# FoX and mLSTM attention steps on visible keys only, with mask and maximum in one VectorE operation

## What is computed

```python
# FoX, for one block of 128 queries
logits = jnp.einsum("bqhd,bkhd->bhqk", qi, k) * scale
logits = logits + (cum_i[..., :, None] - cum[..., None, :])
logits = jnp.where(q_pos[:, None] >= key_pos[None, :], logits, -jnp.inf)
p = jax.nn.softmax(logits, axis=-1)
...
# mLSTM; the kernel takes all 256 tokens as one chunk
dmat = cum[..., :, None] - cum[..., None, :] + ig[..., None, :]
dmat = jnp.where(causal, dmat, -jnp.inf)
m_t = jnp.maximum(inter, jnp.max(dmat, axis=-1))
s = jnp.einsum("bhtd,bhsd->bhts", qb, kb) * jnp.exp(dmat - m_t[..., None])
den = jnp.sum(s, axis=-1) + ...
h_out = num / jnp.maximum(jnp.abs(den), jnp.exp(-m_t))[..., None]
```

## Time and profile before

| | |
|---|---|
| median of three runs | 2455.86 us (2450.93, 2455.86, 2457.76) |
| profiled execution | 2448.87 us, of which the span of the trace is 2447.1 us |
| TensorE busy | 2365.3 us, 97% of the span |
| VectorE busy | 1998.9 us, 82% |
| ScalarE busy | 1032.1 us, 42% |
| mean granted TensorE clock | 0.993 of full |
| where FoX stands in the span | about 203.7 to 316.8 us |
| where mLSTM stands | about 316.8 to 386 us |

### The profile page before, as it was taken

The page is one execution under the profiler, slowest core; times in us unless marked ns, Lnnn a source line. Parts: engine busy times, 40 slices in busy tenths (PEclk is TensorE's granted clock), DMA queues, the critical chain, the costliest instruction groups (busy, mean ns, idle before and its releaser), DMA issues.

```text
span 2447.1 us, 33588 instructions
## 1 busy us (share of the span) xinstructions
PE 2365.3 (97%) x12586; PEld 2029.7 (83%) x12586; DVE 1998.9 (82%) x2707; ACT 1032.1 (42%) x1116; POOL 12.4 (1%) x23
## 2 busy tenths in 40 slices
PE   6999989899999999999989999998999999999998
PEld 6878877788888888888778888887888888888886
DVE  6779987889988888888878888877888678877875
ACT  2134444454433444344455444544444333433343
POOL 0000000000000000000000000000000000000000
PEclk9999999999999999999999999999999999999999
DMA  9999966857798667966858665565555755576553
GB/s 399 413 370 360 347 248 238 312 198 267 258 346 326 237 234 278 363 234 225 331 196 315 233 221 192 186 259 193 187 189 209 289 209 186 189 268 232 187 189 138
DMA packets 114465, 627.00 MB, mean 256 GB/s; under 512 B 12768, under 2 KB 12960, under 8 KB 63152
## 3 DMA queue, kind: packets, MB, share of 16 engines
q1 hardware_dynamic: 113648, 621.22, 68.6%
q10 hardware_dynamic: 704, 4.23, 0.4%
HBM read 623.27 MB, written 2.13 MB: 256 GB/s over the span
## 4 chain that ended last, share of the span: by engine, by line
PE 75%; DVE 14%; DMA 7%; ACT 3%; issue 1%; SPq 0%; DVEq 0%; ACTq 0%
PE bank L1825 29%; PE bank L1826 15%; PE bank L1849 9%; PE bank L1851 9%; PE bank L1850 9%; DVE lo L996 5%; DMA region<-ada_pieces 3%; DMA piece<-ada_pieces 2%; DVE piece L1007 2%; ACT hi L566 1%; PE bank L1731 1%; PE bank L1605 1%; DVE region L1007 1%; DVE y L1007 1%; DMA raw<-w_units 1%
## 5 line engine op out<-in xcount | busy, mean ns | idle before, releaser
L1825 PE MATMUL bank<-act,hi 128*128 128x512 f32 x3328 | 1172.1, 397 | 6.9 <-DVE lo L996 5.6
L566 ACT ACTIVATE hi<-raw 128x2048 fp32r<-128x2048 f32 x378 | 723.6, 1915 | 785.1 <-PE bank L1851 413.2
L1826 PE MATMUL bank<-act,lo 128*128 128x256 f32 x3616 | 1015.1, 281 | 0.0
L996 DVE TENSOR_TENSOR lo<-raw,hi 128x2048 fp32r<-128x2048 f32 x378 | 864.8, 2288 | 153.4 <-ACT hi L566 152.9
L1825 PEld LDWEIGHTS bank<-act,hi 128*128 128x128 f32 x3328 | 624.2, 188 | 159.2 <-DVE lo L996 7.0
L1826 PEld LDWEIGHTS bank<-act,lo 128*128 128x128 f32 x3616 | 685.0, 189 | 0.2
L1849 PE MATMUL bank<-hi,mid 128*128 128x512 f32 x704 | 274.5, 390 | 3.1 <-DVE lo L996 3.1
L1851 PE MATMUL bank<-hi,mid 128*128 128x512 f32 x704 | 274.0, 389 | 0.0
L1850 PE MATMUL bank<-lo,mid 128*128 128x512 f32 x704 | 274.0, 389 | 0.0
L1007 DVE SCALAR_TENSOR_TENSOR piece<-piece,cond 128x1024 f32<-128x1024 f32 x203 | 246.5, 1219 | 14.3 <-DMA piece<-ada_pieces 13.9
L1849 PE MATMUL bank<-hi,act 128*128 128x512 f32 x512 | 203.6, 398 | 6.3 <-DVE lo L996 4.0
(11 more groups left out here) (183 smaller groups left out, 1855.4 us busy)
## 6 DMA issues: line engine op xcount, KB each, us to landing
raw<-w_units SPq DMA_DIRECT2D x378, 1024.0 KB, 4.9
piece<-ada_pieces SPq DMA_DIRECT2D x203, 512.0 KB, 5.7
region<-ada_pieces SPq DMA_DIRECT2D x124, 512.0 KB, 7.9
y<-ada_pieces SPq DMA_DIRECT2D x46, 512.0 KB, 5.7
raw<-head_units SPq DMA_DIRECT2D x16, 1024.0 KB, 16.0
extra<-ada_pieces SPq DMA_DIRECT2D x11, 512.0 KB, 5.8
region<-gamma_scratch ACTq DMA_DIRECT2D x4, 1024.0 KB, 7.0
x<-x_in SPq DMA_DIRECT2D x1, 2048.0 KB, 9.4
```

What stands on the lines that cost most here:

```text
L566: sc.activation(hi[:, slot, :], raw[:, raw_slot, :], ACT.Copy).then_inc(s_hi, 1)
L996: ve.tensor_tensor(lo[:, slot, :], raw[:, raw_slot, :], hi[:, slot, :].bitcast(F32), ALU.subtract).then_inc(s_lo, 1)
L1825: pe.matmul(both, w_hi, act[:, kt, :], start=at == 0, stop=False)
L1826: i_ = pe.matmul(dst, w_lo, act[:, kt, 0:T], start=False, stop=at == DK - 1)
```

## The change

Every step of both attentions is cut to `seen(tb)` keys, 128 for token block 0 and 256 for block 1: the row product, the mLSTM scores, the mask and maximum, the exponential, the product with the scores and the scaling. (The FoX scores, the transposes and the attention products were cut already.) The row product, one matmul of 512 columns before, becomes two of 128 and 256. The mask addition and the maximum, two VectorE operations over 512 columns with a wait between them, become one `tensor_tensor_reduce` for each token block. For mLSTM its start value 0.0 takes over the `min` with 0.0 that the negation did.

```diff
-OWN = {("ff_up", None): 8, ("columns", "fox"): 4, ("values", "fox"): 8, ("columns", "mlstm"): 14,
+OWN = {("ff_up", None): 8, ("columns", "fox"): 2, ("values", "fox"): 4, ("columns", "mlstm"): 12,
...
+def seen(tb):
+
+    return (tb + 1) * P
...
-        def row_twice(k):
-
-            return extra[:, (1 + k) * T:(2 + k) * T].unsqueeze(1).broadcast_to([P, TB, T])
+        def row(k, size=T, rows=GATES):
+            return extra[0:rows, (1 + k) * T:(1 + k) * T + size]
...
-                    i_ = sc.activation(l_[:, tb, :], l_[:, tb, :], ACT.Copy, scale=column(at_ + tb))
+                    i_ = sc.activation(l_[:, tb, 0:seen(tb)], l_[:, tb, 0:seen(tb)], ACT.Copy, scale=column(at_ + tb))
...
-                                i_ = sc.activation(m_l(k)[:, tb, :], m_l(k)[:, tb, :], ACT.Exp,
-                                                   bias=column(8 * k + tb))
+                                l_ = m_l(k)[:, tb, 0:seen(tb)]
+                                i_ = sc.activation(l_, l_, ACT.Exp, bias=column(8 * k + tb))
...
-            def masked_max(l_, bank_, at_):
-
-                ve.tensor_tensor(l_, split2(bank_[:, :]), causal[:, :, :], ALU.add).then_inc(s_v, own.tick())
-                mine()
-                ve.tensor_reduce(stat[:, at_:at_ + 2], l_, AX_X, ALU.max).then_inc(s_v, own.tick())
+            def masked_max(l_, bank_, at_, least):
+
+                for tb in range(TB):
+                    i_ = ve.tensor_tensor_reduce(l_[:, tb, 0:seen(tb)], bank_[:, tb * T:tb * T + seen(tb)],
+                                                 causal[:, tb, 0:seen(tb)], 1.0, least, ALU.add, ALU.max,
+                                                 stat[:, at_ + tb:at_ + tb + 1])
+                i_.then_inc(s_v, own.tick())
                 mine()
...
-                        masked_max(m_l(k), bank[4 + 2 * k], 8 * k)
-                        ve.tensor_scalar(stat[:, 8 * k:8 * k + 2], stat[:, 8 * k:8 * k + 2], -1.0, 0.0, ALU.mult,
-                                         ALU.min).then_inc(s["mlstm_max_ready"], 1)
+                        masked_max(m_l(k), bank[4 + 2 * k], 8 * k, 0.0)
+                        ve.tensor_scalar(stat[:, 8 * k:8 * k + 2], stat[:, 8 * k:8 * k + 2], -1.0, None,
+                                         ALU.mult).then_inc(s["mlstm_max_ready"], 1)
...
-                            i_ = ve.tensor_tensor_reduce(m_l(k)[:, tb, :], m_l(k)[:, tb, :],
-                                                         bank[5 + 2 * k][:, tb * T:(tb + 1) * T], 1.0, 0.0, ALU.mult,
+                            l_ = m_l(k)[:, tb, 0:seen(tb)]
+                            i_ = ve.tensor_tensor_reduce(l_, l_,
+                                                         bank[5 + 2 * k][:, tb * T:tb * T + seen(tb)], 1.0, 0.0, ALU.mult,
...
+            def row_products(to, k, closes):
+
+                for tb in range(TB):
+                    pe.matmul(to[:, tb * T:tb * T + seen(tb)], ones[:, 0:P], row(k, seen(tb), P), start=tb == 0,
+                              stop=closes and tb == TB - 1)
...
-                        pe.matmul(split2(bank[4 + k][:, :]), ones[:, 0:P], row_twice(k), start=True, stop=False)
+                        row_products(bank[4 + k], k, False)
...
-                        pe.matmul(split2(bank[4 + 2 * k][:, :]), ones[:, 0:P], row_twice(k), start=True, stop=True)
+                        row_products(bank[4 + 2 * k], k, True)
...
-                            i_ = pe.matmul(bank[5 + 2 * k][:, tb * T:(tb + 1) * T], m_q(k)[:, tb * P:(tb + 1) * P],
-                                           region[:, bass.ds((MK + k) * T + i * 2 * T, T)], start=True, stop=True)
+                            i_ = pe.matmul(bank[5 + 2 * k][:, tb * T:tb * T + seen(tb)], m_q(k)[:, tb * P:(tb + 1) * P],
+                                           region[:, bass.ds((MK + k) * T + i * 2 * T, seen(tb))], start=tb == 0,
+                                           stop=tb == TB - 1)
```

More of the change, by code:

```diff
@@ L323, in program @@
         gate_rows = extra[0:GATES, 0:T]
-        def row(k):
-            return extra[0:GATES, (1 + k) * T:(2 + k) * T]
-        def row_twice(k):
-            return extra[:, (1 + k) * T:(2 + k) * T].unsqueeze(1).broadcast_to([P, TB, T])
+        def row(k, size=T, rows=GATES):
+            return extra[0:rows, (1 + k) * T:(1 + k) * T + size]
         def fox_part(k, a, b):
@@ L726, in after_split @@
                             for tb in range(TB):
-                                i_ = sc.activation(fox_l(k)[:, tb, :], fox_l(k)[:, tb, :], ACT.Exp,
+                                l_ = fox_l(k)[:, tb, 0:seen(tb)]
+                                i_ = sc.activation(l_, l_, ACT.Exp,
                                                    bias=column(4 * k + tb), accum_out=column(4 * k + 2 + tb))
@@ L1187, in normed @@
                 for tb in range(TB):
-                    i_ = ve.tensor_scalar(l_[:, tb, :], l_[:, tb, :], stat[:, at_ + tb:at_ + tb + 1], None, ALU.mult)
-                return i_
-            def masked_max(l_, bank_, at_):
-                ve.tensor_tensor(l_, split2(bank_[:, :]), causal[:, :, :], ALU.add).then_inc(s_v, own.tick())
-                mine()
-                ve.tensor_reduce(stat[:, at_:at_ + 2], l_, AX_X, ALU.max).then_inc(s_v, own.tick())
+                    i_ = ve.tensor_scalar(l_[:, tb, 0:seen(tb)], l_[:, tb, 0:seen(tb)], stat[:, at_ + tb:at_ + tb + 1], None,
+                                          ALU.mult)
+                return i_
+            def masked_max(l_, bank_, at_, least):
[4 more added lines that the diff above has]
+                i_.then_inc(s_v, own.tick())
                 mine()
@@ L1240, in after_split @@
                             ve.wait_ge(s["fox_scores_ready"], done)
-                            masked_max(fox_l(k), bank[4 + k], 4 * k)
+                            masked_max(fox_l(k), bank[4 + k], 4 * k, NEG)
                             ve.tensor_scalar(stat[:, 4 * k:4 * k + 2], stat[:, 4 * k:4 * k + 2], -1.0, None, ALU.mult)\
@@ L1670, in fox_work @@
                         pe.wait_ge(s["fox_row_ready"], done)
-                        pe.matmul(split2(bank[4 + k][:, :]), ones[:, 0:P], row_twice(k), start=True, stop=False)
+                        row_products(bank[4 + k], k, False)
                         for tb in range(TB):
-                            seen = (tb + 1) * P
-                            i_ = pe.matmul(bank[4 + k][:, tb * T:tb * T + seen], fox_q(k)[:, tb * P:(tb + 1) * P],
-                                           region[:, bass.ds((FK + k + 2 * pair) * T, seen)], start=False,
+                            i_ = pe.matmul(bank[4 + k][:, tb * T:tb * T + seen(tb)], fox_q(k)[:, tb * P:(tb + 1) * P],
+                                           region[:, bass.ds((FK + k + 2 * pair) * T, seen(tb))], start=False,
                                            stop=tb == TB - 1)
```

## The result

The changed kernel took 2439.43 us (median of 20 executions, 2430.89 to 2446.99) against 2451.83 us for the kernel before (20 executions, 2443.56 to 2457.98). The ratio is 0.995, with an interval of 0.9942 to 0.9959: 12.3 us faster, 10 to 14. That is double the 6.2 us forecast, and outside the range given. "Within 0.3%" was called likeliest, and it was 0.5%. The kernel before is itself 4.0 us lower here, with twenty executions, than the 2455.86 us of three from which the forecast was counted down. The profiled execution took 2441.35 us, its span 2439.6 us.

The account below looks back on a forecast made before the run. It took TensorE and VectorE, both full in FoX, and TensorE's wait for VectorE's weights in mLSTM as the bounds. FoX 3.5 plus mLSTM 2.7 made 6.2 us, from 2455.86 to 2449.7 us, range 2443.5 to 2455.

Parts of the forecast that it names:

- Within 0.3%: Whole kernel: a result within 0.3% of the time before was given 0.53, faster 0.42, slower 0.05.
- Mask and maximum: VectorE, mask to negation: 1.44 us a head falls to 0.66, saving 0.78, or 6.2 in eight FoX heads.
- The half rate: VectorE's new operation: if it ran at half rate, 0.42 us more a head, and the sum 4.5 instead of 6.2.
- Products: TensorE's row products in FoX: 0.85 us falls to 0.66 a head, 1.5 us in eight heads; mLSTM scores counted at nothing.
- FoX, TensorE's waits: FoX: TensorE's waits for ScalarE's weights and a low part vanish, 1.1 + 0.2 = 1.3 us.
- 0.7 for spacing: FoX upper bound: 0.7 us more for spacing that modelled ends hide, making 4.2 instead of 3.5 us.
- VectorE's relief beyond TensorE's pace: FoX: TensorE sets the pace, so 2.7 of VectorE's 6.2 us saved become idle time.
- The end of FoX: End of FoX: VectorE's lateness for the last copy vanishes, 0.7 us, and the next stage starts sooner.
- mLSTM: First mask to second scaling: 6.87 us falls to 5.52, VectorE waiting some 0.6 for ScalarE; 2.7 saved in two bodies.
- The clock: Rival, chance 0.31: clock stays up around the second mLSTM transposes, 1.85 us more, sum 8.0, 2447.8 us.
- The other rivals: DMA feeds FoX no faster, 2451.7 us (0.18); products no cheaper, 2451.2 (0.05); maximum form of the operation slower, 2466 (0.04).
- The range: Whole kernel: bounds of the terms 3.7 to 7.3 us, up to 2446.2 with the clock, widened to 2443.5 and 2455.

Follow-up runs that it names:

- fused_whole: Kernel before with mask and maximum fused into one VectorE operation per token block, still over all 256 keys in both blocks: 2447.04 us, ratio 0.9971.
- dve_only: Changed kernel with TensorE's row and score products left whole as before, so only VectorE's and ScalarE's work is changed: 2443.26 us, ratio 0.9946.
- before_hold: Kernel before with 28 unused products in TensorE's waits for the mLSTM weights, in both bodies: 2448.2 us, ratio 0.9966.
- clock_hold: Changed kernel with 13 unused products in TensorE's weight waits of the second mLSTM body: 2438.94 us, ratio 0.9924; again (clock_hold_again) 2437.57 us, 0.9932.
- pe_only: Changed kernel with VectorE and ScalarE working as before, so only TensorE's products are cut: 2452.45 us, ratio 0.9989.
- mlstm_only: Changed kernel with the FoX steps as in the kernel before, so the change is in the mLSTM heads alone: 2443.36 us, ratio 0.9974.
- cut_two_ops: Changed kernel with mask and maximum as separate operations again, over the visible keys only: 2446.11 us, ratio 0.9974.
- before_fourth: Kernel before, unchanged, timed again for a fourth profile: ratio 0.9997.
- before_third: Kernel before, unchanged, timed again for a third profile: ratio 0.9991.
- Padded: Changed kernel with 39 unused TensorE products between the attention product and the squares of the second mLSTM body: 2449.07 us, ratio 0.997.
- before_again: Kernel before, unchanged, timed again for a second profile: ratio 0.9999.

## Why the prediction was right and wrong

**Mask and maximum: right.** 0.67 us against 0.66 forecast. fused_whole shows the element's part as forecast: its 128 columns more cost 0.14 us, 1.1 ns each. The half rate that the Trainium skill (Vector Engine (DVE) Microarchitecture Reference, section 7) states is for two sources in SBUF, and the new operation reads one from PSUM, so this does not test it; the row that does is still L1007's, 1.22 us for 1024 columns, which stands against it and is 1.22 us in the changed kernel too (L1009).

**Products: right.** 0.65 us each against 0.66.

**FoX, TensorE's waits: mis-sized, and the largest error that the profiles show.** This is the step of the prediction that failed. It put "its waits of 1.1 + 0.2 = 1.3 us". What the change gave back was twice that. TensorE around the first pair's transposes, before:

```profile
218.10 0.28 PE L1826 MATMUL bank<-act,lo 128*128 128x256 f32 x1
219.06 0.55 PE L1659 MATMUL bank<-ident,region 128*128 128x128 f32 x3 [0.68 <-ACT region L716]
219.86 0.55 PE L1659 MATMUL bank<-ident,region 128*128 128x128 f32 x3 [0.25 <-ACT region L716]
220.37 0.38 PE L1821 MATMUL bank<-act,hi 128*128 128x256 f32 x1
```

And after the change:

```profile
218.99 0.29 PE L1837 MATMUL bank<-act,lo 128*128 128x256 f32 x1
219.11 0.86 PE L1665 MATMUL bank<-ident,region 128*128 128x128 f32 x6
220.15 0.39 PE L1832 MATMUL bank<-act,hi 128*128 128x256 f32 x1 [0.17 <-DVE lo L998]
```

From the last unit product to the next one: 2.27 us before (218.10 to 220.37), 1.16 after. That is 1.11 us given back, where the brackets of before show 0.93. In the other pairs, whose waits are mostly too short to be listed, the same distance went from 1.33, 1.17 and 1.54 to 0.70, 0.81 and 0.81. All four together: 6.31 to 3.48, so 2.8 us. The other three profiles of before give 6.03, 6.55 and 5.92, those of the changed kernel 3.49 each, so 2.7 in the means, and dve_only, with the products as before, 3.07: 3.2 us back, all that its stage got. The modelled end of a matmul covers the first tenths of every stall, and I had put this at "0.7 for spacing" only in the upper bound. 1.5 + 2.8 is 4.3 of the 4.49 us measured. That VectorE's relief beyond TensorE's pace is lost (2.7 us in the forecast) was right in kind: 6.2 us saved on VectorE, 4.5 of the stage. But it did not become idle time, as the forecast had it: that is 3.0 us before and 3.1 after.

**The end of FoX: right.** The first mLSTM mask starts 5.62 us behind the stage's row product before (322.40 − 316.78) and 4.73 after (318.31 − 313.58), so 0.9 us against 0.7.

**mLSTM: right.** 5.53 us against 5.52, with the wait for ScalarE at 0.49 against 0.6. The first body came out shorter by 2.24 us, which is 1.34 and these 0.9. The second gained 1.65. In this pair of profiles its clock fall was 6.8 us long before and 3.4 after, so a part is the clock's, about 0.3 by the 1.35 that are left with no fall on either side (29.68 in before_hold, 28.33 in clock_hold). In the means of four the second body gained 1.1.

**The clock: the wrong fall was looked at.** The rival expected the wait before the second transposes to become short enough. It fell from 3.77 to 2.62 us, and the clock fell all the same, in all four profiles of the changed kernel (in one of them for 3.4 us, in three for 6.8 as in all four of before). What the change removed was another fall, in the first body, that the profile of before did not have. It came in four of six profiles in which VectorE's FoX work was as before and no products filled the waits (two of before's four, pe_only, mlstm_only), and in none of the eleven with that work shorter, cut_two_ops with its 0.14 us a head among them. It costs 1.2 to 1.9 us (37.38 and 37.63 against 36.17 and 35.75), so about 0.8 in the mean of before. Why VectorE's FoX work decides it is argued only: the first body's mask starts 0.9 us sooner. The length of the idle time by itself does not sort the profiles: between the unit products on both sides of the first body's transposes lie 3.87 us in before, where the clock held, and 3.31 in mlstm_only, where it fell.

**The other rivals: fallen.** The DMA engines gave 375 and 389 GB/s at shares of 0.99 and 0.98, more than the 370 that the pair needed, and VectorE waited 0.2 us for a piece in all of FoX: a busy share of 96% was not a limit yet. The operation was not slower for a maximum, and the products did get cheaper.

**The sum.** 4.4 us of FoX and 3.9 of mLSTM (68.3 to 64.4 in the means of four) are 8.3 us against 6.2. This is shown: of the 2.1 us between, TensorE's stalls in FoX are 1.4 to 1.5, and the rest is small terms to both sides, the clock's 0.8 among them. From 8.3 to 12.3 us stays open. What is behind the stages gave 1.0 us in the means, within its scatter. Part is sampling: the four profiled executions of before took 2449.1 us in the mean, 2.6 below the mean of the four medians that they belong to (the executions: 2448.87, 2450.37, 2453.39, 2443.85), while those of the changed kernel, 2440.2, lie on theirs. Taken at that, the profiled executions differ by 8.9 us, and one more like before_fourth or before_third would move this by a microsecond or two. Padded, mlstm_only and before_hold, too, gained 4 to 8 us more in the timing than in their stages, and all ten variants gained more, from 0.9 (fused_whole) to 8.2 (clock_hold). These are not ten witnesses: each is counted from the same four profiles of before, whose 2449.1 us in the mean lie 2.2 to 6.3 below the medians of before (2451.4 to 2455.4) that the ratios are taken against. So if those four happened to be quick ones, all ten surpluses follow at once. That is the likeliest account, but it is argued, not shown: no profile of a slower execution of before says which stretch is longer in it. What is behind the stages can move by enough for it: 2068.1 us in clock_hold and 2058.3 in clock_hold_again, the same kernel twice. Clock falls outside the profiled executions are at most a part: the granted clock is 0.9925 in the mean of the changed kernel's 38 timed executions, 0.9920 in the 36 of before_again, before_third and before_fourth, and 0.9914 in those that the ratios are taken against, which is 1.1 to 2.6 us of clock time, and the falls in the profiled stages are 1.3 of it.

**The range.** It missed for two reasons of about equal size. The forecast was counted down from 2455.86 us, the median of three executions, and twenty have 2451.83: 4.0 of the 10.3 us between 2449.7 and 2439.43. The other 6.2 are the gain, 12.4 between the medians instead of 6.2. The range was made from the bounds of terms that one profile gave, 7.3 us at most without the clock, and I had not allowed for stalls that the rows do not list. (Its lower end with the clock, 2446.2, should have been 2446.7, by 7.3 + 1.85; it decides nothing.) From a base of 2451.83 the same range would end at 2439.5, and the result would still be outside, if barely.

**The best version** is clock_hold: ratios 0.9924 and 0.9932 against 0.995, 0.9949, 0.995 and 0.9952 for the changed kernel, and 4.7 us between the medians where both ran on one chip. Its stages explain 2.2 of these (173.1 to 170.9). The first pair of ratios is apart beyond the intervals (0.991 to 0.9937 against 0.9942 to 0.9959), the second is not (0.9913 to 0.995 against 0.9935 to 0.9969).

## What to carry to other kernels

Where two engines are full, cost both and take the slower: the cheaper products alone gave 0.8 us, VectorE's relief alone 3.2, both together 4.4, and fusing two passes over the same tile gave far more than cutting its columns (0.63 and 0.14 us a head), since it takes away a whole pass of 512 columns and a wait, where the cut takes a quarter of each pass. Read a stall of TensorE from the distance between the starts of the neighbouring products, not from the list of waits, which had 1.1 us where 2.8 came back. And take more than one profile of a kernel, and more than three executions for its median, before arguing from a few microseconds: a clock fall that came in half of the executions was no part of the one that I had read.

## What the runs showed of the hardware that was not expected

- The DMA engines moved 361 GB/s at a busy share of 96% in the second FoX pair before and 375 at 99% after the change, and in the third pair 357 at 94% and then 389 at 98%: at such shares 4 and 9% more was still to be had.
- Filling TensorE's waits with 13 unused products of 128 columns removed a stretch of 1.2 GHz, in two profiles of two, and the body became 1.3 to 2.6 us shorter. The Trainium skill (TensorE: Matmul & The Clock Gate, Part 1) says that the slow level is the default and activity releases it; the trace agrees, with 1.00 instead of 0.50 granted in that stretch.
- The fall after the same wait is 3.4 us long in one execution of the changed kernel and 6.8 in the other three, and its second mLSTM body took 29.7 us with the short one and 30.5 to 30.95 with the long.
